# Sliding-window attention over bands of 192 keys per chunk, and the first output tile gated inside the stick-breaking stage

## The chip, the cores and the metric

The kernel runs on one core of a Trainium2 chip. The metric is the device time of one execution in microseconds (us), the median of several runs. A profile, taken by the hardware on one execution, gives for every instruction its engine, start and duration, and for every stretch the granted clock of TensorE. The engines are PE (TensorE matmul; its weight loads are shown apart as PEld), DVE (VectorE), ACT (ScalarE), POOL (GpSimd) and SP (SyncE, which here only issues DMAs).

## What is computed

One layer of a streaming encoder on 2048 prompt rows with 16 meta rows ahead of them, and 32 sample rows. The input projection gives the operands of three mixers (A, B, C) and a gate z; the mixers' outputs are joined, gated and projected back. The change touches mixer A (attention in which a chunk of 64 rows sees its own chunk and the two before it) and the joining at the end:

```
WIN_CHUNKS = WINDOW // CHUNK            # 128 // 64 = 2
def swa_prompt(q, k, v, sinks):
    ...
    band = lambda a: jnp.concatenate([a[:, j:j + n_c] for j in range(WIN_CHUNKS + 1)], axis=2)
    k_band = band(to_chunks(k))         # per chunk of 64 rows: 3 * 64 = 192 keys
    v_band = band(to_chunks(v))
    ...
    o = sink_attention(qc, k_band, v_band, sinks, ok)

def mixer_output(h, o_a, o_b, o_c, z, g_post, w_out):
    o = jnp.concatenate([o_a, o_b, o_c], axis=-1) * jax.nn.silu(z)
    return h + rmsnorm(jnp.einsum('btm,md->btd', o, w_out), g_post)
```

Mixer B is stick-breaking attention over all earlier rows, mixer C a gated delta rule.

## The kernel before, in words

The 2128 rows lie in 17 row tiles of 128 (TILES = 17, P = 128), so one tile holds two chunks of 64 (CH). The program is a row of stages, each with its own instruction streams per engine and a barrier between: the projection and convolution, the delta rule (both with side projections woven in), `window_attention`, `stick_breaking`, `output`. Within a stage the order of work on an engine is as written; engines meet by semaphores.

**`window_attention`** walks over `units` (m, s): row tile m (0 to 16, and 17 for the sample rows) and s, one of two sets of 4 heads, so 36 units. In step n, PE does `scores(n)`, `turn(n-3)` and `values(n-4)`. `scores` (L1474) first writes the mask of the window into PSUM `b_sc` by two matmuls of an identity with a mask table (L1486: 512 columns each, for two heads), then adds q times k for 4 heads (L1493: 64 contracted rows, 128 query rows, 256 keys, that is the row tile before and its own). DVE takes the row maximum (L1596) and forms the bias `nm` (L1600) and `se` (L1603); ACT does the exponentials with their sums, one per head (L1554), POOL multiplies by the reciprocal sum (L1580), PE turns the probabilities on their side (L1510, 128x128, 8 per unit) into `b_pt`, ACT (L1565) and DVE (L1626) copy one half each of that into `pt`, and `values` multiplies by v (L1524) into `b_o`, which DVE copies out per row tile (L1631). DVE's order in step n is maximum, `nm` and `se` of unit n, copy of unit n-3, then the sum and the reciprocal (L1610, L1614) of unit n-1, which release POOL. In fp32 each product is issued as two passes, a transpose as one.

**`stick_breaking`** runs 92 steps; in each, PE makes scores (L1816), transposes (L1839) and value products (L1854), ACT a sigmoid (L1907) and copies (L1921), DVE two scans (L1967). POOL only stores finished blocks of 4 row tiles into the scratch tensor `mix` (L1939). Towards its end SP loads `w_out` piece by piece into `w_raw` (L1788), a view of `base`.

**`output`** takes 17 row tiles through: SP loads the tile's `mix` and `sz` (gate) columns and the residual (L2047, L2048, L2056); ACT makes sigmoid(z) (L2089), POOL z times it (L2159), DVE gates `mixed` (L2128), ACT and DVE split the result into a high and a low part (`mhi` L2094, `mlo` L2132), and PE makes 48 passes of 512 columns (L2078). The weights are split likewise at the stage's start, k by k (`whi` L2115, `wlo` L2147), with the work on tile 0 written in between:

```
for k in range(KT):
    act.activation(whi[:, k, :], w_raw[:, k, :], ACT.Copy).then_inc(w_hi, 1)
    if k == SPLIT0 - 1:
        z_sigmoid(0, 0, 0)
    if k == SPLIT0:
        high(0, 0, 0)
z_sigmoid(1, 1, 0)
steps(act, step)
```

From then on ACT's `step` for tile n is z_sigmoid(n+2), a table load, high(n+1), and the normalisation of tile n.

Of the kernel before, what the change touches and what calls it, by code (L numbers as in the profile page):

```python
# [62 lines left out]
M_ID, M_DT, M_A0, M_A1, M_A, M_B = 0, 128, 192, 320, 576, 832  # L63
# [3 lines left out]
def shape_constants():  # L67
# [22 lines left out]
    cb[:, M_A:M_A + 2 * P] = np.where(win, 0, NEG)  # L90
# [6 lines left out]
def stream_layer(nc, io):  # L97
    top = ExitStack()
    with top:
# [24 lines left out]

        u_first = base_flat[:, 0:5 * P].rearrange("p (k t) -> p k t", k=5)
# [1273 lines left out]
        def window_attention():  # L1399
# [3 lines left out]
            with ExitStack() as st:  # L1403
# [5 lines left out]
                pr = sb("pr", [P, 4, AG, 2 * P], st=st)  # L1409
                pt = sb("pt", [P, 2, 2, AG, P], st=st)  # L1410
# [15 lines left out]
                slots = [(j, u) for u in range(2) for j in range(AKV)]  # L1426
                N = len(units)
# [17 lines left out]
                with nc.Block() as block:  # L1445
                    @block.sync
                    def _(sp):
# [4 lines left out]
                        load_piece(0)  # L1452
                        sp.dma_start(kc[:, :], io["cache_a_k"][0, 0].rearrange("t h d -> t (h d)")).then_inc(cache_in, 16)
# [19 lines left out]
                    def _(pe):  # L1473
                        def scores(n):  # L1474
# [7 lines left out]
                            q0 = SROW if m == TILES else m * P  # L1482
                            for a in range(0, AG, 2):
                                if m < TILES:
                                    at = M_A0 if m == 0 else (M_A1 if m == 1 else M_A)
                                    pe.matmul(b_sc[:, n % 2, a:a + 2, 0:K], identb, wide(cb[:, at:at + K], 2), start=True, stop=False,  # L1486
                                              skip_group_check=True)
# [12 lines left out]
                        def turn(n):  # L1500
# [3 lines left out]
                            if n:  # L1504
                                pe.wait_ge(pt_kept_act, n)
                                pe.wait_ge(pt_kept_dve, n)
                            for t, (_, part, k0) in enumerate(key_tiles(m, 0)):
# [5 lines left out]
                        def values(n):  # L1513
# [4 lines left out]
                            if n >= 4 and s == 0:  # L1518
                                pe.wait_ge(o_kept, n // 2 - 1)
                            heads = [key_tiles(m, j) for j in range(AKV)]  # L1520
# [128 lines left out]
        def stick_breaking():  # L1649
# [6 lines left out]
            TURN, VALUE = 3, 5  # L1656
            QS, KS = 0, 4
            with ExitStack() as st:
# [13 lines left out]
                krow = sb("krow", [P, 2, 2 * VBW], st=st)  # L1672
                spilled = [sem(f"spilled{b}", st) for b in range(NBLK)]
# [83 lines left out]
                with nc.Block() as block:  # L1757
                    @block.sync
                    def _(sp):
# [21 lines left out]
                        pieces += [(w_raw[:, k, :], wo[k * P:(k + 1) * P, :]) for k in range(AG, KT)]  # L1781
# [118 lines left out]
                    def _(act):  # L1900
# [15 lines left out]
                        for s in range(N + TURN):  # L1916
                            if s < N and s % 2 == 0:
# [330 lines left out]
```

## Time and profile before

| | us |
|---|---|
| runs | 1541.35, 1536.29, 1537.98 |
| median | 1537.98 |
| profiled execution, its own time | 1535.92 |
| its span, first to last instruction | 1534.2 |
| window_attention, about | 914.7 to 1047 |
| stick_breaking, about | 1051 to 1313 |
| output, about | 1317 to 1534 |

The page gives busy times per engine; the timeline gives start and duration of single instructions or of runs of like ones; the windows give the busy time of each engine in a stretch, with the granted clock (1.00 is 2.4 GHz, 0.50 is 1.2 GHz). A matmul's shown duration holds the pipeline's depth, so the rate of PE is read from start to start, not from durations.

### The profile page before, as it was taken

To read this page: it belongs to the slowest core of one execution; us is meant where nothing else is said; L and a number is where in the kernel's file an instruction comes from. 1 tells how busy PE (TensorE), PEld (TensorE's weight loads), DVE (VectorE), ACT (ScalarE), POOL (GpSimd) and SP (SyncE) were. 2 spreads that over 40 slices of the span, in tenths; PEclk is the share of its full clock that TensorE was granted. 3 is DMA by queue.
4 is the path that set the end of the run, shared out by engine and by line. 5 is a ranking of instruction groups with operands and counts; after the bars stand their busy time and mean duration, and the time that the engine had idled before them with its cause. 6 is when DMAs were issued, how large, how long until landed. Compare 5 with 4: busy or idle time off the path is not lost. (4 is left out here: it accounts for less than half of the span.)

```text
span 1534.2 us, 31162 instructions
## 1 busy us (share of the span) xinstructions
PE 1438.6 (94%) x12700; PEld 1196.5 (78%) x12700; DVE 792.2 (52%) x1507; ACT 640.9 (42%) x1440; POOL 383.8 (25%) x364
## 2 busy tenths in 40 slices
PE   6999998879999999999999979997999999599996
PEld 5999998868888888888888965554666666487785
DVE  5665566313334333335333327776788887444442
ACT  4455455411222112113111117674666676455551
POOL 0022223212212222223222114551000000255553
PEclk9999999899999999999999989998999999799998
DMA  8554446394243244433344423133000014656651
GB/s 249 169 149 130 142 124 160 106 224 135 83 132 97 68 117 125 127 94 96 110 126 126 121 73 120 64 102 94 15 15 2 15 33 122 189 158 170 201 177 62
DMA packets 202224, 177.36 MB, mean 116 GB/s; under 512 B 30114, under 2 KB 187879, under 8 KB 202087
## 3 DMA queue, kind: packets, MB, share of 16 engines
q1 hardware_dynamic: 153385, 117.86, 26.1%
q0 software_dynamic: 28256, 46.42, 10.9%
q10 hardware_dynamic: 20446, 11.14, 2.9%
q8 instruction: 99, 1.62, 0.4%
q14 instruction: 38, 0.31, 0.1%
HBM read 107.92 MB, written 65.59 MB: 113 GB/s over the span
## 5 line engine op out<-in xcount | busy, mean ns | idle before, releaser
L817 PE MATMUL acc<-side_rows,side_w 128*128 128x384 f32 (+2 forms) x2448 | 457.4, 335 | 15.9 <-ACT side_stage L836 7.7
L817 PEld LDWEIGHTS acc<-side_rows,side_w 128*128 128x128 f32 x2448 | 393.0, 191 | 33.3 <-ACT side_stage L836 7.8
L1967 DVE TENSOR_TENSOR_SCAN prod<-keepb,prod 128x512 f32<-128x512 f32 (+4 forms) x184 | 195.6, 1104 | 52.6 <-ACT keepb L1907 45.1
L709 PE MATMUL acc<-side_rows,side_w 128*128 128x384 f32 (+1 forms) x864 | 149.3, 330 | 0.0
L1276 DVE COPY base<-b_two 128x256 f32<-128x256 f32 x85 | 36.1, 424 | 212.9 <-PE b_two L1067 212.9
L709 PEld LDWEIGHTS acc<-side_rows,side_w 128*128 128x128 f32 x864 | 142.4, 188 | 1.9
L836 ACT ACTIVATE side_stage<-acc 128x384 f32<-128x384 f32 (+2 forms) x102 | 46.8, 461 | 211.4 <-PE acc L817 186.9
L2078 PE MATMUL b_y<-whi,mhi 128*128 128x512 f32 x272 | 107.4, 395 | 20.6 <-DVE mlo L2132 20.5
L1921 ACT ACTIVATE wt<-b_w 128x512 f32<-128x512 f32 (+5 forms) x188 | 88.0, 521 | 61.2 <-PE b_w L1839 61.1
L2078 PE MATMUL b_y<-whi,mlo 128*128 128x512 f32 x272 | 106.4, 391 | 0.0
L2078 PE MATMUL b_y<-wlo,mhi 128*128 128x512 f32 x272 | 106.4, 391 | 0.0
L1001 POOL TENSOR_TENSOR base<-base,ors 128x256 f32<-128x256 f32 x17 | 10.4, 611 | 334.9 <-ACT ors L1232 334.9
L1183 ACT ACTIVATE base<-b_dr 128x256 f32<-128x256 f32 x85 | 32.5, 383 | 144.5 <-PE b_dr L1059 144.5
L1907 ACT ACTIVATE keepb<-b_z 128x1024 f32<-128x1024 f32 (+4 forms) x92 | 79.7, 890 | 30.1 <-PE b_z L1816 18.9
L994 POOL TENSOR_TENSOR base<-base,cf 128x256 f32<-128x256 f32 x102 | 72.3, 743 | 79.2 <-DVE base L1257 79.2
L1839 PE MATMUL b_w<-cf,prod 128*128 128x128 f32 (+1 forms) x624 | 87.4, 280 | 3.1 <-ACT wt L1921 2.0
L1816 PE MATMUL b_z<-reg 64*128 64x512 f32 (+3 forms) x360 | 85.1, 575 | 4.4 <-PEq L2191 4.4
L1839 PEld LDWEIGHTS b_w<-cf,prod 128*128 128x128 f32 (+1 forms) x624 | 66.9, 142 | 27.2 <-issue 23.3
L1854 PE MATMUL b_o<-wt,vrow 128*64 128x128 f32 x1224 | 78.5, 278 | 6.5 <-DVE reg L1974 6.5
L1580 POOL TENSOR_TENSOR pr<-pr,rd 128x1024 f32<-128x1024 f32 (+2 forms) x36 | 65.1, 1809 | 68.5 <-ACT pr L1554 53.9
L2078 PEld LDWEIGHTS b_y<-whi,mhi 128*128 128x128 f32 x272 | 51.4, 189 | 34.6 <-DVE mlo L2132 19.5
L1854 PEld LDWEIGHTS b_o<-wt,vrow 128*64 128x64 f32 x1224 | 66.4, 137 | 15.0 <-issue 13.7
(230 smaller groups left out, 2345.9 us busy)
## 6 DMA issues: line engine op xcount, KB each, us to landing
side_rows<-hs_scratch POOLq DMA_DIRECT2D x16, 1536.0 KB, 10.3
hs_scratch<-side_rows SPq DMA_DIRECT2D x34, 512.0 KB, 4.7
mixed<-mix_scratch SPq DMA_DIRECT2D x17, 512.0 KB, 6.5
gates<-sz_scratch SPq DMA_DIRECT2D x17, 512.0 KB, 8.1
side_rows<-hs_scratch POOLq DMA_DIRECT2D x6, 1344.0 KB, 10.6
base<-in_x_prompt SPq DMA_DIRECT2D x15, 512.0 KB
xres<-in_x_prompt SPq DMA_DIRECT2D x15, 512.0 KB
out_y_prompt<-yy POOLq DMA_DIRECT2D x15, 512.0 KB, 6.5
```

The costliest lines, as they stand in the source:

```text
L709: last = pe.matmul(acc[:, u % 2, 0:w], side.w[:, c, w_, k, :], h_[:, b % 2, k, 0:w], start=(k == 0 and p == 0), stop=(k == KT - 1 and p == 2))
L817: last = pe.matmul(self.acc[:, n % 2, 0:width], w[:, w_part, k, :], rows[:, row_part, k, 0:width], start=(k == 0 and i == 0), stop=(k == K ...
L836: act.activation(self.stage[:, n % 2, 0:width], self.acc[:, n % 2, 0:width], ACT.Copy).then_inc(self.staged, 1)
L994: pool.tensor_tensor(atl[:, l], at[:, :, :], wide(lvl(l), 4), ALU.mult).then_inc(level, 1)
L1580: pool.tensor_tensor(x, x, rd[0:R, n % 4, :].unsqueeze(2).to_broadcast([R, AG, K]), ALU.mult).then_inc(normed, 1)
L1816: last = pe.matmul(b_z[0:R, s % 2, hh, 0:nk], reg[half, QS + a, q0:q0 + R], reg[half, KS + a, k0:k0 + nk], start=True, stop=not masks, ski ...
L1839: last = pe.transpose(b_w[0:kn, hh, t, 0:R], prod[0:R, hh, c0 + at:c0 + at + kn], ident[0:R, 0:R])
L1854: last = pe.matmul(b_o[hh * CH:hh * CH + CH, rowno[s] % 2, 0:R], v, wt[part, s % 4, hh, t, 0:R], start=(first and t == 0), stop=(last_ and ...
L1907: act.activation(keepb[0:R, s % 2, :, 0:nk], b_z[0:R, s % 2, :, 0:nk], ACT.Sigmoid, scale=-SCALE).then_inc(keep_ready, 1)
L1921: keep_weights(act, s - TURN, hh, lambda o, i: act.activation(o, i, ACT.Copy))
L1967: dve.tensor_tensor_scan(prod[0:R, hh, c0:c0 + nk][:, ::-1], kv, kv, prod[0:R, hh, c0 + nk:c0 + nk + 1], ALU.mult, ALU.bypass).then_inc(pr ...
L2078: last = pe.matmul(b_y[:, s, cols], m_[:, s, k, :], w_[:, k, cols], start=(k == 0 and p == 0), stop=(k == KT - 1 and p == 2))
```

## The change

Two things. For row tiles 2 to 16 ("banded", 30 of the 36 units) `window_attention` no longer computes 128 queries against 256 keys with a mask; each half tile (chunk c of 64 queries) is multiplied with its own band of 192 keys, which needs no mask. The scores become 8 products of 64 contracted rows, 64 query rows and 192 keys, one in each of the four quarters of the array for u and again; the transposes become 8 of 64 rows into 128x64 and 8 of 64 rows into 64x64; the values become, for each chunk, two products with 128 contracted rows and two with 64. Chunk 1's last 64 keys lie in partitions 64 to 127 of `vrow`, so a copy `v_low` in partitions 0 to 63 is made by one DMA at the stage's start. ACT's exponentials, DVE's maximum and POOL's product work on 192 instead of 256 columns per head. Tiles 0, 1 and the sample keep the old form.

Second, row tile 0 of the output is gated in `stick_breaking`: SP loads its `sz` and, once block 0 is stored, its `mix` columns into parts of `w_raw` not yet filled; ACT makes the sigmoid in step 41 (GATE), POOL two products of 128x1024. The last of the 8 pieces of `w_out` (k = 7) is loaded only in `output`, after tile 0 is split. `output` starts with high(0) and low(0), its first load is tile 1's, and PE does tile 0 k by k for both column halves.

```
 def window_attention():
+                v_low = sb("v_low", [CH, TILES, P], st=st)
...
+                b_band = b_pt[:, :, :, :].rearrange("p c g k -> p c (g k)").rearrange("p c (t g k) -> p c t g k", t=2, g=AG)
...
                 def keys(m):
-                    return P if m == 0 else (WIN + NSAMP if m == TILES else 2 * P)
+                    return P if m == 0 else (WIN + NSAMP if m == TILES else (2 * P if m == 1 else BAND))
...
                         load_piece(0)
+                        sp.dma_start(v_low[:, :, :], vA[CH:P, :, 0:P]).then_inc(low_in, 16)
...
+                            if banded(m):
+                                for u in range(2):
+                                    for c in range(2):
+                                        for j in range(AKV):
+                                            k0 = (m - 1) * P + c * CH
+                                            last = pe.matmul(b_sc[halves[c], n % 2, 2 * j + u, 0:BAND], reg[half[j], 2 * s + u, q0 + c * CH:q0 + (c + 1) * CH],
+                                                             reg[half[j], 4, k0:k0 + BAND], start=True, stop=True)
+                                last.then_inc(scores_ready, 1)
+                                return
...
+                            if banded(m):
+                                for g in range(AG):
+                                    for c in range(2):
+                                        pe.transpose(b_band[:, c, 0, g, :], pr[halves[c], n % 4, g, c * CH:c * CH + P], ident[halves[c], halves[c]])
+                                for g in range(AG):
+                                    for c in range(2):
+                                        k0 = 0 if c else P
+                                        last = pe.transpose(b_band[0:CH, c, 1, g, :], pr[halves[c], n % 4, g, k0:k0 + CH], ident[halves[c], halves[c]])
...
+                                for c in range(2):
+                                    for j in range(AKV):
+                                        pe.matmul(b_o[halves[j], m % 2, 2 * s:2 * s + 2, halves[c]], vA[:, m - 1 + c, halves[j]],
+                                                  p_band[:, n % 2, c, 0, 2 * j:2 * j + 2, :], start=True, stop=False)
+                                    for j in range(AKV):
+                                        rest = v_low[:, m - 1, halves[j]] if c else vA[0:CH, m, halves[j]]
+                                        last = pe.matmul(b_o[halves[j], m % 2, 2 * s:2 * s + 2, halves[c]], rest,
+                                                         p_band[0:CH, n % 2, c, 1, 2 * j:2 * j + 2, :], start=False, stop=True)
 def stick_breaking():
+            GATE = 41
...
+                        sp.dma_start(gate_raw, sz[:, :, 0:P].rearrange("k p t -> p k t")).then_inc(first_in, 16)
+                        sp.wait_ge(first_stored, 16)
+                        sp.dma_start(gated_first, mix[:, :, 0:P].rearrange("k p t -> p k t")).then_inc(first_in, 16)
+                        sp.wait_ge(first_gated, 1)
...
                         for s in range(N + TURN):
+                            if s == GATE:
+                                act.wait_ge(first_in, 32)
+                                act.activation(gate_sig, gate_raw, ACT.Sigmoid).then_inc(first_sig, 1)
...
                             store_outputs(b, 4 * (b + 1))
+                            if b == 1:
+                                pool.wait_ge(first_sig, 1)
+                                pool.tensor_tensor(gate_raw, gate_raw, gate_sig, ALU.mult).then_inc(first_silu, 1)
+                                pool.wait_ge(first_silu, 1)
+                                pool.tensor_tensor(gated_first, gated_first, gate_raw, ALU.mult).then_inc(first_gated, 1)
 def output():
...
+                            if exact(n) and n == 0:
+                                load(*ahead(1))
+                                sp.wait_ge(m_lo, 1)
+                                sp.dma_start(w_raw[:, KT - 1, :], io["w_out"][0][(KT - 1) * P:KT * P, :]).then_inc(w_last_in, 16)
+                                sp.dma_start(gpost[:, :], io["norm_post"].to_broadcast([P, D])).then_inc(gpost_in, 16)
+                            elif not exact(n) or n > 1:
+                                load(n, s, q)
+                            load_x(n, s, q)
...
+                        high(0, 0, 0)
                         for k in range(KT):
+                            if k == KT - 1:
+                                act.wait_ge(w_last_in, 16)
                             act.activation(whi[:, k, :], w_raw[:, k, :], ACT.Copy).then_inc(w_hi, 1)
-                            if k == SPLIT0 - 1:
-                                z_sigmoid(0, 0, 0)
-                            if k == SPLIT0:
-                                high(0, 0, 0)
-                        z_sigmoid(1, 1, 0)
+                            if k == SPLIT1:
+                                z_sigmoid(1, 1, 0)
```

How this stands on the engines: first PE in the middle of `window_attention`, one step of the loop before (scores, turn, values; a row is output, inputs and the product's shape):

```order
L1486 MATMUL b_sc<-cb 128x512 x2
L1493 MATMUL b_sc<-reg 128x256 x4
L1510 MATMUL b_pt<-cf,pr 128x128 x8
L1524 MATMUL b_o<-pt,vrow 64x256 x4
L1486 MATMUL b_sc<-cb 128x512 x2
```

and the same step now:

```order
L1499 MATMUL b_sc<-reg 64x192 x8
L1530 MATMUL b_pt<-cf,pr 128x64 x8
L1534 MATMUL b_pt<-cf,pr 64x64 x8
L1555 MATMUL b_o<-pt,vrow 64x2x64 x2
L1559 MATMUL b_o<-pt,vrow 64x2x64 x2
L1555 MATMUL b_o<-pt,vrow 64x2x64 x2
L1559 MATMUL b_o<-pt,v_low 64x2x64 x2
```

The 18 instructions of a step have become 32, the two of the mask are gone, and the values now go to and fro between 128 contracted rows (L1555) and 64 (L1559).

ACT at the start of `output`, before:

```order
L2115 ACTIVATE whi<-base 128x1024 x5
L2089 ACTIVATE zsig<-gates 128x1024
L2115 ACTIVATE whi<-base 128x1024
L2094 ACTIVATE mhi<-mixed 128x1024
L2115 ACTIVATE whi<-base 128x1024 x2
L2089 ACTIVATE zsig<-gates 128x1024 x2
L2109 ACT_TABLE_LOAD
L2094 ACTIVATE mhi<-mixed 128x1024
```

and now:

```order
L2172 ACTIVATE mhi<-base 128x1024
L2196 ACTIVATE whi<-base 128x1024 x6
L2166 ACTIVATE zsig<-gates 128x1024
L2196 ACTIVATE whi<-base 128x1024 x2
L2166 ACTIVATE zsig<-gates 128x1024
L2187 ACT_TABLE_LOAD
L2172 ACTIVATE mhi<-mixed 128x1024
```

Tile 0's sigmoid is gone and its high part stands first; the high part of tile 1 still stands behind the sigmoid of tile 2 and a table load.

SP at the start of `output`, before:

```order
L2047 DMA mixed<-mix_scratch 128x8x128
L2048 DMA gates<-sz_scratch 128x8x128
L2051 DMA xres<-in_x_prompt 64x1024
L2061 DMA gpost<-in_norm_post 128x1024
L2047 DMA mixed<-mix_scratch 128x8x128
L2048 DMA gates<-sz_scratch 128x8x128
L2056 DMA xres<-in_x_prompt 128x1024
L2047 DMA mixed<-mix_scratch 128x8x128
L2048 DMA gates<-sz_scratch 128x8x128
```

and now:

```order
L2108 DMA mixed<-mix_scratch 128x8x128
L2109 DMA gates<-sz_scratch 128x8x128
L2126 DMA base<-in_w_out 128x1024
L2127 DMA gpost<-in_norm_post 128x1024
L2114 DMA xres<-in_x_prompt 64x1024
L2119 DMA xres<-in_x_prompt 128x1024
L2108 DMA mixed<-mix_scratch 128x8x128
L2109 DMA gates<-sz_scratch 128x8x128
```

The first pair is tile 1's now, the second tile 2's; one pair less and the last piece of the weights more stand ahead of the gates of tile 2.

## Rows read from the trace of the kernel before

**Rows 1.** The page: busy us, share of the span and instructions of each engine.

```profile
PE 1438.6 (94%) x12700; PEld 1196.5 (78%) x12700; DVE 792.2 (52%) x1507; ACT 640.9 (42%) x1440; POOL 383.8 (25%) x364
```

**Rows 2.** Windows: stretch, its length, busy us of each engine, granted clock, DMA share, GB/s.

```profile
940.00:968.40 28.40, 28.40 (x206) 16.99 (x206) 20.80 (x52) 19.37 (x78) 15.14 (x8) 1.00 0.04 15
...
1160.00:1180.00 20.00, 20.00 (x188) 13.59 (x186) 17.16 (x18) 13.10 (x20) 0.00 (x0) 1.00 0.01 2
...
1313.50:1331.00 17.50, 0.00 (x0) 0.00 (x0) 9.37 (x9) 9.19 (x10) 3.03 (x2) 0.60 0.80 218
1331.00:1343.00 12.00, 11.97 (x47) 9.83 (x48) 5.51 (x4) 4.96 (x5) 6.14 (x2) 0.87 0.74 197
```

**Rows 3.** Timeline of PE in window_attention: start us, duration, engine, line, operation, count.

```profile
926.44 0.60 PE L1486 MATMUL b_sc<-cb 128*128 128x512 bf16 x2 [0.46 <-ACT pr L1554]
...
968.82 0.61 PE L1486 MATMUL b_sc<-cb 128*128 128x512 bf16 x2
...
969.36 1.13 PE L1493 MATMUL b_sc<-reg 64*128 64x256 f32 x8
...
970.42 1.09 PE L1510 MATMUL b_pt<-cf,pr 128*128 128x128 f32 x8
...
971.45 1.08 PE L1524 MATMUL b_o<-pt,vrow 128*64 128x256 f32 x8
...
972.46 0.61 PE L1486 MATMUL b_sc<-cb 128*128 128x512 bf16 x2
...
1034.34 0.41 PE L1496 MATMUL b_sc<-kcT,reg 64*32 64x128 f32 x4
```

**Rows 4.** Instructions on the tile pr: duration ns min/median/max, first and last start, forms.

```profile
L1580 POOL TENSOR_TENSOR pr<-pr,rd x36: 1035/1892/1894, 919.8 to 1043.3; 128x1024 f32<-128x1024 f32 x32, 128x512 f32<-128x512 f32 x2, 32x640 f32<-32x640 f32 x2
```

**Rows 5.** Timeline of DVE and POOL at the end of window_attention.

```profile
1033.68 0.16 DVE L1600 SCALAR_TENSOR_TENSOR nm<-mx,nsink 128x4 f32<-128x4 f32 x1
...
1036.00 0.97 DVE L1600 SCALAR_TENSOR_TENSOR nm<-mx,nsink 32x4 f32<-32x4 f32 x1
...
1038.20 1.89 POOL L1580 TENSOR_TENSOR pr<-pr,rd 128x1024 f32<-128x1024 f32 x1 [1.24 <-DVE rd L1614]
...
1039.39 0.72 DVE L1600 SCALAR_TENSOR_TENSOR nm<-mx,nsink 32x4 f32<-32x4 f32 x1
```

**Rows 6.** Timeline of PE: quarters in the delta rule, halves in the other stages.

```profile
703.86 0.46 PE L1067 MATMUL b_two<-base 64*64 64x64 f32 x16
704.16 0.51 PE L1094 MATMUL b_s<-cx_S,qk_ring 64*64 64x64 f32 x11
...
1045.04 0.34 PE L1524 MATMUL b_o<-pt,vc 128*64 128x64 f32 x4
...
1045.31 0.33 PE L1524 MATMUL b_o<-pt,vrow 32*64 32x64 f32 x4
...
1290.41 1.97 PE L1854 MATMUL b_o<-wt,vrow 128*64 128x128 f32 x32
```

**Rows 7.** Timeline at the start of output.

```profile
1317.21 4.84 ACT L2115 ACTIVATE whi<-base 128x1024 fp32r<-128x1024 f32 x5 [5.68 <-PEq L2191]
...
1318.30 5.77 DVE L2147 TENSOR_TENSOR wlo<-base,whi 128x1024 fp32r<-128x1024 f32 x5 [5.12 <-ACT whi L2115]
...
1323.81 1.06 ACT L2089 ACTIVATE zsig<-gates 128x1024 f32<-128x1024 f32 x1 [1.76 <-DMA gates<-sz_scratch]
...
1324.96 2.33 POOL L2159 TENSOR_TENSOR gates<-gates,zsig 128x1024 f32<-128x1024 f32 x1 [10.76 <-ACT zsig L2089]
...
1331.03 0.80 PE L2078 MATMUL b_y<-whi,mhi 128*128 128x512 f32 x1 [18.15 <-DVE mlo L2132]
...
1334.69 1.06 ACT L2089 ACTIVATE zsig<-gates 128x1024 f32<-128x1024 f32 x1 [2.13 <-DMA gates<-sz_scratch]
...
1338.15 2.04 DVE L2132 TENSOR_TENSOR mlo<-mixed,mhi 128x1024 fp32r<-128x1024 f32 x1 [1.30 <-ACT mhi L2094]
...
1343.42 0.39 PE L2078 MATMUL b_y<-whi,mhi 128*128 128x512 f32 x1
```

More of the change, by code:

```diff
@@ L2011, in output @@
                 LOOPS = (TILES - 8) // 3
-                SPLIT0 = 5
+                SPLIT1 = 5
+                w_last_in = sem("w_last_in", st)
                 mixed, gates = (sb(n, [P, 3, KT, P], st=st) for n in ("mixed", "gates"))
@@ L2016, in output @@
                 exact = lambda n: isinstance(n, int)
+                landed = lambda s, q: 32 * q + (32 if s else 0)
                 def rows(ap, n, base):
@@ L2071, in step, with products @@
                             reuse(pe, normed, n)
-                            for c in range(2):
+                            def products(k, c):
                                 cols = slice(c * 512, (c + 1) * 512)
-                                for k in range(KT):
-                                    if exact(n) and n == 0 and c == 0:
-                                        pe.wait_ge(w_lo, k + 1)
-                                    for p, (m_, w_) in enumerate(((mhi, whi), (mhi, wlo), (mlo, whi))):
-                                        last = pe.matmul(b_y[:, s, cols], m_[:, s, k, :], w_[:, k, cols],
-                                                         start=(k == 0 and p == 0), stop=(k == KT - 1 and p == 2))
+                                for p, (m_, w_) in enumerate(((mhi, whi), (mhi, wlo), (mlo, whi))):
+                                    last = pe.matmul(b_y[:, s, cols], m_[:, s, k, :], w_[:, k, cols],
+                                                     start=(k == 0 and p == 0), stop=(k == KT - 1 and p == 2))
+                                return last
+                            if exact(n) and n == 0:
+                                for k in range(KT):
+                                    pe.wait_ge(w_lo, k + 1)
+                                    for c in range(2):
+                                        last = products(k, c)
+                            else:
+                                for c in range(2):
+                                    for k in range(KT):
+                                        last = products(k, c)
                             last.then_inc(y_ready, 1)
@@ L2143, in step @@
                             norm(*ahead(0))
+                        low(0, 0, 0)
                         for k in range(KT):
```

57 lines of the change are left out of this document (35 added, 22 removed).

## The prediction

> **What bounds the kernel now.** I read the page first: PE is busy for 94% of the span [rows 1], so the end is set by PE's queue nearly everywhere, and a step is worth what it takes off PE, as long as no other engine is late next. Then the windows: in the middle of window attention PE is busy all 28.4 of 28.4 us at full clock, while DVE, the busiest beside it, has 20.8 [rows 2]. The other place is the head of the output stage: for 17.5 us PE does nothing [rows 2]; its first product starts at 1331.03, 13.8 us after ACT began on the weights [rows 7]. The change works on these two places, and borrows from a third, stick-breaking, where PE is busy 20.0 of 20.0 us and DVE 17.2 [rows 2].
>
> One step of window attention, from start to start on PE [rows 3]: masks 0.54 (968.82 to 969.36), scores 1.06, transposes 1.03, values 1.01; together 3.64. The 30 units that the change rewrites begin with the masks at 926.44 and end where the sample's scores begin, 1034.34: 107.9 us, 3.60 each (the first three are shorter).
>
> **The masks** go: minus 0.54 per unit, certain.
>
> **The scores** are now 16 passes of 192 columns in quarters of the array. Before, 8 passes of 256, two halves abreast, took 1.06 with everything around them, 0.52 ns per column. If four quarters run abreast, 3072 columns take 3072 x 0.26 = 0.80; if only two do, 1.59. The delta rule shows quarters: 16 passes of 64 columns (L1067) start at 703.86 and the next group starts 0.30 later [rows 6], 0.29 ns per column with short passes, which is close to 0.26. I take 0.80.
>
> **The transposes** keep their 1024 columns (16 of 64 for 8 of 128), now in two row halves that may run abreast: 0.51 if they do, 1.03 if not. No row shows fp32 transposes of two halves side by side, and there are twice as many weight loads, so I take 0.70.
>
> **The values** keep their columns too: 16 passes of 128. The nearest row is stick-breaking's, the same shape, 32 passes in 1.97 [rows 6], so 0.99. But a unit now goes three times between 128 and 64 contracted rows. The price of such a change: at the sample's units four passes of 64 columns with 128 rows start at 1045.04 and the four with 32 rows 0.27 later [rows 6]; by the rate above those passes need 4 x 31 ns = 0.12, so 0.15 is the change of form. Three of them are 0.45, and I take 0.36 of it, since some are covered by weight loads that run ahead: 1.35 (ends 0.99 and 1.44).
>
> The Trainium skill, "TensorEngine Tiling (Array Packing)", section "Key Properties", says that changing the tiling mode drains TensorE, and speaks against this change; the 0.15 above agrees with it. By that rule alone the sum would be 1.44 for the values and 0.15 more before the transposes.
>
> PE per unit: 0.80 + 0.70 + 1.35 = 2.85 (ends 0.80 + 0.51 + 0.99 = 2.30 and 1.59 + 1.03 + 1.44 = 4.06).
>
> **What is late next in window attention** is a loop of DVE and POOL. At the end of the stage, where no masks stand in PE's queue, DVE's small `nm` takes 0.97 and 0.72 instead of 0.16 [rows 5], and ends with POOL's product: POOL runs from 1038.20 to 1040.09, `nm` ends at 1040.11. `nm` waits for POOL, and POOL waits for what DVE does after `nm` (`se`, copy, sum, reciprocal): from 1036.97 to 1038.20, 1.23. So a step can't be shorter than 1.23 + POOL's 1.89 + 0.02 = 3.14 before. POOL takes 1.89 for 1024 columns and 1.03 for 512 [rows 4], so 1.46 for 768: 2.71 after. That lies just under PE's 2.85; ACT's and DVE's own work shrink as well. I take 2.85 for the step, which PE sets, with 2.71 as the floor: 30 x 2.85 = 85.5, **minus 22.4** (minus 26.6 at the floor).
>
> **`v_low`** is one DMA of 64 x 17 x 512 bytes, 0.56 MB, put ahead of the cache and the later pieces in SP's queue. It is first needed four steps after the first banded scores, and what is queued behind it is needed in steps 2 and 4. At the 218 GB/s of the output's head [rows 2] it is 2.6 us; mostly covered by units 0 to 2: plus 0.3 (0 to 2.6).
>
> **The output's head.** Tile 0 no longer waits for its loads, sigmoid and gate. High part from 1317.21, 1.06; low part 1.2; the first `wlo` 1.2 more (`whi` and `wlo` come at 4.84 / 5 = 0.97 and 5.77 / 5 = 1.15 each [rows 7]); so PE starts at about 1320.7 instead of 1331.03. Tile 0 takes 12.4 (1331.03 to 1343.42 [rows 7]), needs a new k only every 1.5 us, and would end at 1333.1. But tile 1 isn't ready then: its high part stands behind the sigmoid of tile 2 on ACT, and that waits for the gates, which landed at 1334.69, 17.5 us after the first load was issued [rows 7]. Ahead of them stand 3.75 MB now instead of 4.25 (one pair of 0.5 MB less, one piece of weights more), so 15.4 us: 1332.6. From there to the end of `mlo` it was 5.5 (1334.69 to 1340.19 [rows 7]): tile 1 starts at 1338.1 instead of 1343.42, 5.3 earlier, not 10.3. And PE has then stood still for 5.0 us. In the head before, the clock fell while PE stood still (mean 0.60 over 17.5 us, thus 3.5 us at 2.4 GHz and the rest at 1.2), and after PE's restart 3.1 of 12 us ran at 1.2 GHz (mean 0.87) [rows 2], which costs half of that. I count it a second time, at tile 1: 1.5. Gain 5.3 - 1.5 = 3.8 (ends: 1.7 if the gates land no earlier, 6 with no fall of the clock). The later tiles follow PE by a chain that starts from PE's own ends, so the gain stays to the end.
>
> **In stick-breaking** the gate adds 1.06 on ACT (as at 1323.81 [rows 7]) and two products of 2.33 on POOL [rows 7], idle until then. SP's wait for POOL delays only stores and weights that are due much later; POOL's next store, of block 2, has time. DVE is another matter, since its scans read SBUF while POOL does: in window attention `nm` stood still for POOL [rows 5], and at the output `mlo` took 2.04 where `wlo` of the same size takes 5.77 / 5 = 1.15 [rows 7]. If both products hold DVE up fully, that is 4.7 us in a stage where DVE is idle 14% of the time; with ACT's 1.06 the ends are 0 and 5.7. I take 1.5, since PE, two to three steps behind the scores, uses up DVE's lead and idle time first. **Gate in all: minus 2.3.**
>
> **Sum.** -22.4 + 0.3 - 2.3 = -24.4. The profiled execution's own time is 1535.92, so 1511.5; the median of the runs lies 2.06 above that execution: **1513.5**.
>
> **Rivals.**
> 1. *Slower: parts of the array do not run abreast.* If only two quarters do, and the transposes go one by one, PE needs 4.06 per unit: 30 x 4.06 = 121.8, plus 13.9, and with the gate 1549.6. It decides from a PE sum of 3.60 per unit. Against it: the quarters of the delta rule [rows 6]. Chance 0.06.
> 2. *Changes of form eat the gain.* Scores four abreast, transposes one by one (1.03), values 1.44: 3.27, and 0.15 more at one edge of the group: 3.4 per unit, minus 5.9; with the rest 1530. For it: 32 instructions for 18. Against: in two row halves the scores already ran abreast. Chance 0.14, of which a third within 0.3%.
> 3. *The gate costs more than it gives.* Both POOL products stop the scans, 5.7 lost in stick-breaking against 3.8: plus 1.9, 1517.7. Chance 0.15. The Trainium skill, "SBUF — State Buffer", section "SBUF: two separate sides", has such a rule: a GpSimd operation and a VectorE one with two SBUF inputs exclude each other for the whole instruction, and the scan has two such inputs; `nm` above agrees.
> 4. *The step doesn't shrink with its columns.* POOL's product over four strips of 192 costs what 1024 contiguous columns cost, and the loop stays at 3.14: 94.2, minus 13.7; 1522. For it: no row has a time for strips with gaps between. Against it: the two sizes in [rows 4] scale with their columns, and the gaps are in the free dimension alone. Chance 0.07.
>
> **How the numbers follow.** The forecast has 0.58. A measurement of this kernel can tell 0.3%, 4.6 us, from no change. Faster by more: 0.58 + 0.15 + 0.07 + two thirds of 0.14 = 0.89; within: 0.05; slower: 0.06. The range reaches down to 1503 (loop at its floor, minus 26.6, gate at its best, minus 6, and 2 us in the median) and up to 1527 (PE at 3.25 per unit, minus 10.4, and the gate without gain); rival 1 and most of rival 2 stay outside.
>
> **What would show it.** In the profile after: the step in the middle of window attention about 2.85 from start to start; 16 passes of scores in 0.8, transposes in 0.7, values in 1.35; `nm` often ending with POOL's product, which takes 1.46; PE's first product of the output some 3.5 us after ACT's first instruction there (13.8 before), then a gap of about 5 us ahead of tile 1, with the clock down; the scans next to POOL's two products stretched. A step over 3.3 or under 2.7, a tile 1 that starts without a gap, or a stick-breaking stage longer by more than 5 us would make steps of this wrong.

## The result, and the profile after

The changed kernel takes 1512.41 us (median of 4 runs, 1510.33 to 1515.72) where the kernel before takes 1537.13 beside it (4 runs, 1535.9 to 1541.35): a ratio of 0.984, 95% interval 0.9824 to 0.9857. That is faster by 24.7 us; 1513.5 had been forecast, in a range of 1503 to 1527. The profiled execution has a span of 1508.7 us against 1534.2. The page's line of the engines, to be read against [rows 1] (busy us, share of the span, instructions):

```profile
PE 1416.8 (94%) x13360; PEld 1190.4 (79%) x13360; DVE 771.9 (51%) x1506; ACT 636.3 (42%) x1440; POOL 377.4 (25%) x365
```

PE is busy 21.8 us less and still for 94% of the span. By stage, each measured between the same first instructions on PE and ACT in both traces:

| stretch | before | after | difference |
|---|---|---|---|
| up to window attention | 914.8 | 915.1 | +0.3 |
| window attention, up to the first banded scores | 11.7 | 12.4 | +0.7 |
| the 30 banded units | 107.9 | 83.7 | -24.2 |
| the sample's units and the change to the next stage | 16.6 | 16.1 | -0.6 |
| stick-breaking | 266.2 | 268.6 | +2.4 |
| output, from ACT's first piece of it | 217.0 | 212.9 | -4.2 |

Windows of after (stretch, length, busy us of each engine with its instructions, granted clock, DMA share, GB/s): the middle of window attention, the place of the gate in stick-breaking, and two stretches of the output's head. They answer to [rows 2].

```profile
940.00:967.20 27.20, 27.09 (x480) 18.00 (x474) 25.72 (x66) 23.40 (x102) 14.66 (x10) 1.00 0.21 63
1130.00:1150.00 20.00, 18.46 (x185) 12.76 (x182) 19.72 (x18) 13.58 (x21) 5.54 (x2) 1.00 0.00 1
1295.80:1313.00 17.20, 13.41 (x48) 10.57 (x48) 11.54 (x10) 10.82 (x12) 6.01 (x2) 0.75 1.00 290
1313.00:1326.00 13.00, 9.52 (x35) 7.66 (x36) 4.87 (x4) 8.34 (x10) 8.60 (x4) 0.87 0.43 111
```

The 27.20 us of the first row hold ten banded steps. PE is full, as before, but DVE now stands at 25.7 of 27.2, where it had 20.8 of 28.4: two limits have come to lie side by side. One step on PE, from transposes to transposes (start, duration, engine, line, operation, tile form, which is the rows*columns of the array in use, shape, count):

```profile
962.48 0.47 PE L1530 MATMUL b_pt<-cf,pr 64*128 64x64 f32 x8
962.78 0.39 PE L1534 MATMUL b_pt<-cf,pr 64*64 64x64 f32 x8
963.10 0.44 PE L1555 MATMUL b_o<-pt,vrow 128*64 128x128 f32 x4
963.47 0.44 PE L1559 MATMUL b_o<-pt,vrow 64*64 64x128 f32 x4
963.84 0.44 PE L1555 MATMUL b_o<-pt,vrow 128*64 128x128 f32 x4
964.21 0.33 PE L1559 MATMUL b_o<-pt,v_low 64*64 64x128 f32 x2
...
964.23 0.39 PE L1499 MATMUL b_sc<-reg 64*64 64x192 f32 x2
...
965.22 0.47 PE L1530 MATMUL b_pt<-cf,pr 64*128 64x64 f32 x8
```

From start to start it is 2.74 instead of the 3.64 of [rows 3]: transposes 0.62 (962.48 to 963.10), values 1.13 (to 964.23, where the next scores start while the last values still run), scores 0.99 (to 965.22; from 964.44 on, alone, 14 passes in 0.78). POOL's product, which answers to [rows 4] (min/median/max ns), is the other limit:

```profile
L1623 POOL TENSOR_TENSOR pr<-pr,rd x36: 1033/1467/1893, 920.1 to 1018.6; 128x768 f32<-128x768 f32 x30, 128x512 f32<-128x512 f32 x2, 128x1024 f32<-128x1024 f32 x2, 32x640 f32<-32x640 f32 x2
```

1.47 for 768 columns. Its starts in the banded steps lie 2.71 to 2.74 apart, 2.72 in the mean, 0.02 less than PE's. The timeline of after at the output's head: ACT, DVE, POOL, and PE's last product of tile 0 and first of tile 1 (compare [rows 7]):

```profile
1295.83 1.06 ACT L2172 ACTIVATE mhi<-base 128x1024 fp32r<-128x1024 f32 x1 [6.02 <-PEq L2266]
...
1298.06 9.17 DVE L2227 TENSOR_TENSOR wlo<-base,whi 128x1024 fp32r<-128x1024 f32 x8
...
1303.61 5.89 POOL L2235 TENSOR_TENSOR gates<-gates,zsig 128x1024 f32<-128x1024 f32 x1 [10.85 <-ACT zsig L2166]
...
1311.74 1.06 ACT L2166 ACTIVATE zsig<-gates 128x1024 f32<-128x1024 f32 x1 [6.33 <-DMA gates<-sz_scratch]
...
1312.45 0.39 PE L2143 MATMUL b_y<-whi,mlo 128*128 128x512 f32 x1
...
1312.82 1.28 ACT L2187 ACT_TABLE_LOAD   x1
1314.11 1.06 ACT L2172 ACTIVATE mhi<-mixed 128x1024 fp32r<-128x1024 f32 x1
...
1315.20 1.23 DVE L2210 TENSOR_TENSOR mlo<-mixed,mhi 128x1024 fp32r<-128x1024 f32 x1 [4.34 <-ACT mhi L2172]
...
1316.48 0.50 PE L2143 MATMUL b_y<-whi,mhi 128*128 128x512 f32 x1 [3.65 <-DVE mlo L2210]
...
1318.05 0.63 PE L2143 MATMUL b_y<-whi,mhi 128*128 128x512 f32 x1
```

PE's first product of the output is at 1299.43, 3.6 us after ACT's first piece (13.8 before). The gap of 3.65 ahead of tile 1 is the one foreseen: the high part of tile 1 stands on ACT behind the sigmoid of tile 2, which waits 6.33 for its gates. Some 1.5 us into tile 1 the products double in spacing, 0.43 instead of 0.23; the clock was 0.87 in this window, and tile 1 took 12.7 us where the next took 10.9.

### The profile page after: what moved, and what is told of

The parts are those of the page before. It is cut to its first block and busy times, and to the rows that moved or that the text cites. A ratio compares the mean times of both kernels' runs of the same rounds, so it can differ in the third digit from the quotient of the medians.

```text
span 1508.7 us, 32486 instructions
## 1 busy us (share of the span) xinstructions
PE 1416.8 (94%) x13360; PEld 1190.4 (79%) x13360; DVE 771.9 (51%) x1506; ACT 636.3 (42%) x1440; POOL 377.4 (25%) x365
## 5 line engine op out<-in xcount | busy, mean ns | idle before, releaser
L2026 DVE TENSOR_TENSOR_SCAN prod<-keepb,prod 128x512 f32<-128x512 f32 (+4 forms) x184 | 199.5, 1126 | 50.8 <-ACT keepb L1958 43.2
L695 PE MATMUL acc_v<-wv_hi,side_rows 128*128 128x392 f32 x272 | 74.9, 347 | 2.8 <-DVE side_rows L541 2.1
```

The costliest lines, as they stand in the source:

```text
L695: last = pe.matmul(acc_v[:, 0:RV], h_[:, s, k, part], w_[:, k, :], start=(k == 0 and p == 0), stop=(k == KT - 1 and p == 2))
L2026: dve.tensor_tensor_scan(prod[0:R, hh, c0:c0 + nk][:, ::-1], kv, kv, prod[0:R, hh, c0 + nk:c0 + nk + 1], ALU.mult, ALU.bypass).then_inc(pr ...
```

## The experiments

The theory was the prediction's: a banded step is limited by PE and, close beneath, by the loop of DVE and POOL; the gate gains at the output's head what a gap and a fall of the clock leave of it, and costs something beside the scans. The rivals were that the gate costs as much as it gives, and that one of the two limits alone sets the step.

**The two halves apart.** e1 has the new `window_attention` with `stick_breaking` and `output` as before; e2 the reverse.

```
e1:  stick_breaking, output: the functions of the kernel before
+    gated_first = w_raw[:, KT - 1, :].rearrange("p (k t) -> p k t", k=KT)     (left in e1, not used there)
e2:  window_attention: the function of the kernel before
```

> Bands of 192 keys alone; stick-breaking and output as before. Theory A (the two parts are independent and the trace's split is right: window attention 24.0 us shorter, the gate worth 4.1 - 2.4 = 1.7 net): 24 us under the kernel before, a ratio near 0.984, with window attention about 112 us from its first product to stick-breaking's (136 before) and the other stages within 0.5 us of before. Rival B (part of the output's gain comes from the earlier stage, or the bands disturb what follows): a total that differs from 24 by more than 2 us.

> The gate of tile 0 in stick-breaking alone; window attention as before. Theory A: 1.7 us under the kernel before (2.4 lost in stick-breaking, 4.1 won in output), a ratio near 0.999, hardly told from 1. Rival B (the loss in stick-breaking belongs to the other part): 4 us under. Rival C (the gain at the output's head is given back later): no change or slower.

e1 took 1513.81 us, ratio 0.9859 (0.9841 to 0.9877), e2 1531.56, ratio 0.9972 (0.996 to 0.9984), against 1536.64 beside them. The bands give 22.8 us, as theory A had them (within 2 of 24). The gate alone gives 5.1, more than A's 1.7 and B's 4; together they'd be 27.9, but the changed kernel has 24.7. The stages say where the rest is: stick-breaking loses 1.9 in e2 (268.1) and nothing in e1 (266.4), so the gate costs there what after shows. The output shrinks by 6.6 in e2 (210.4) and by 4.2 in after. In e2 tile 1 starts 19.91 us after ACT's first piece, after a wait of 2.93, and takes 11.0: the granted clock stayed at 1.00. In after it starts at 20.65, after a wait of 3.65, and takes 12.7. So most of the difference of 2.4 between the two outputs, 1.7, is the clock in tile 1.

**POOL's share of the step.** e5 lets POOL multiply only 64 of the 192 columns, so the other probabilities stay unnormalised.

```
-    x = pr[0:R, n % 4, :, 0:K]
+    W = CH if 2 <= m < TILES else K
+    x = pr[0:R, n % 4, :, 0:W]
```

> The changed kernel in which POOL multiplies 64 of the 192 columns per head in the banded units (the other probabilities stay without the division by the sum: part of the computation is left out). POOL's product falls from 1.47 to about 0.65. If PE sets the step: it stays at 2.74, window attention at 112. If the loop of DVE and POOL sets it: nm is no longer held up and the step falls to what DVE needs itself, 2.5 to 2.6, window attention to 105 to 108.

The step stayed at 2.74. What changed is `nm`, the small instruction that follows DVE's maximum. The row of the instructions on `nm` in the middle of window attention in after (count, then min/median/max ns):

```profile
L1643 DVE SCALAR_TENSOR_TENSOR nm<-mx,nsink x25: 161/166/750, 941.6 to 1007.5; 128x4 f32<-128x4 f32 x25
```
and the same row in e5:

```profile
L1644 DVE SCALAR_TENSOR_TENSOR nm<-mx,nsink x26: 161/163/165, 940.9 to 1009.3; 128x4 f32<-128x4 f32 x26
```

With POOL's product at 0.61 us, `nm` is never held (165 ns at most), and the step is no shorter: PE's 2.74 holds it.

**PE's share of the step.** e4 groups the value products by form: all with 128 contracted rows, then all with 64. In this order the sums over the keys of a half are not kept whole, so part of the values is left out; it is read for its time.

```
     for c in range(2):
         for j in range(AKV): ... vA[:, m - 1 + c, halves[j]] ... start=True
+    for c in range(2):
         for j in range(AKV): ... rest ... stop=True
```

> The changed kernel with the values of a unit in another order: the four products with 128 contracted rows first, then the four with 64, so one change of form inside the values where there were three. Against the changed kernel's step of 2.74. If the loop of DVE and POOL is the floor (POOL's 1.47 and 1.25 between its product and the next nm): PE gains 2 x 0.16 but the step stays at 2.71 to 2.74, window attention at about 112. If PE alone sets the step: 2.42, window attention about 102 to 103. If the change of form costs nothing: 2.74 and the values take as long as now, 1.13 up to the next scores.

Here, too, the step hardly moved: 2.72. PE now waits 0.21 us at the transposes for DVE's copy of the step before, and `nm` is held in every second step, up to the end of POOL's product (the same row in e4):

```profile
L1644 DVE SCALAR_TENSOR_TENSOR nm<-mx,nsink x26: 161/457/754, 940.5 to 1009.1; 128x4 f32<-128x4 f32 x26
```

In after, too, `nm` is held in every second step, but for less and less: from 750 ns down to 166, as it must be where the loop needs 0.02 less than PE's step. In e4 it is held for 750 to 754 to the end. So each limit alone holds the step where it is: PE at 2.74, the loop at 2.72.

e4 and e5 ran once each, in 1516.48 and 1516.54 us, and the whole of window attention took 116.4 and 116.9 where about 112 had been expected. That isn't the banded units (83.0 and 83.3 us; 83.0 in e1, 83.7 in after) but what stands around them: the start took 15.2 and 16.6, which comes up again below, and the sample's units with the change of stage 18.2 and 17.0 instead of 16.1, which was not pursued.

**Both limits lifted.** e7 puts the value products in the order 64, 128, 128, 64 rows, which has two changes of form instead of four and adds up each half before the next begins, and lets DVE make the reciprocal ahead of its copy, so that POOL's product runs beside copy and maximum.

```
-    for c in range(2):                    # 128 rows, then 64, for each half
+    for c, wide_step in ((0, False), (0, True), (1, True), (1, False)):
+        opens = (c == 1) == wide_step
...
-    if 3 <= n < N + 3: keep(n - 3)
     if 1 <= n <= N: norm(n - 1)
+    if 3 <= n < N + 3: keep(n - 3)
```

> The changed kernel with both limits of the banded step lifted at once: TensorE's value products in the order 64, 128, 128, 64 rows (two changes of tile form instead of four, sums as before), and VectorE makes the reciprocal ahead of its copy of the transposed probabilities, so that GpSimd's product runs beside copy and maximum. Theory (a step is the larger of TensorE's 2.74 and the VectorE-GpSimd loop's 2.72, and nothing else is near): the step falls to 2.55 to 2.65 us and the stretch of window attention by 2 to 5 us against a run with the same start. Rival (a third limit, ScalarE with 2.30 busy and its wait of 0.42 for the bias): the step stays at 2.70 or more.

POOL's starts now lie 2.74 and 2.38 to 2.59 apart in turn (once 3.11), 2.62 in the mean, inside the 2.55 to 2.65 expected; the 30 units took 80.2 us instead of 83.7, and the one run 1505.64. One step on PE in e7, from its timeline:

```profile
961.17 0.46 PE L1530 MATMUL b_pt<-cf,pr 64*128 64x64 f32 x8
961.44 0.42 PE L1534 MATMUL b_pt<-cf,pr 64*64 64x64 f32 x8
961.79 0.44 PE L1562 MATMUL b_o<-pt,vrow 64*64 64x128 f32 x4
962.15 0.66 PE L1558 MATMUL b_o<-pt,vrow 128*64 128x128 f32 x8
962.74 0.33 PE L1562 MATMUL b_o<-pt,v_low 64*64 64x128 f32 x2
...
963.76 0.46 PE L1530 MATMUL b_pt<-cf,pr 64*128 64x64 f32 x8
```
and the row of `nm` in e7:

```profile
L1645 DVE SCALAR_TENSOR_TENSOR nm<-mx,nsink x27: 149/162/165, 941.3 to 1009.5; 128x4 f32<-128x4 f32 x26, 32x4 f32<-32x4 f32 x1
```

Eight passes of 128 rows in one group take 0.59 (962.15 to 962.74); in after the same eight took 0.37 twice. That prices a change of form at 0.15, as the prediction had it from the sample's units. The step shown fell by one such price, from 2.74 to 2.59, though two changes are gone: the one behind the transposes had cost nothing that could be seen (the sixteen transposes take 0.62 ahead of it in after, and 0.62 in e7 without it). `nm` is no longer held at all.

Stick-breaking was 2.8 us shorter in this run, though nothing in it was changed. 1.0 of it lies in its first 9 us, where the clock came back sooner (1.00 instead of 0.74 in the 5 us that begin some 5 us after the first product). Another 1.6 lie behind a wait of 2.12 for DVE's `reg`, which both kernels have; in after

```profile
1047.68 1.03 PE L1905 MATMUL b_o<-wt,vrow 128*64 128x128 f32 x12 [2.12 <-DVE reg L2033]
1048.64 1.97 PE L1890 MATMUL b_w<-cf,prod 128*128 128x128 f32 x8
1050.54 1.90 PE L1867 MATMUL b_z<-reg 64*128 64x512 f32 x8
```
and in e7:

```profile
1043.43 0.88 PE L1907 MATMUL b_o<-wt,vrow 128*64 128x128 f32 x12 [2.12 <-DVE reg L2035]
1044.24 1.09 PE L1892 MATMUL b_w<-cf,prod 128*128 128x128 f32 x8
1045.26 1.35 PE L1869 MATMUL b_z<-reg 64*128 64x512 f32 x8
```

The granted clock of this piece was 0.64 in after (1047.68 to 1052.37) and 1.00 in e7 (1043.43 to 1046.55). e10 below, with the same edit, shows the same; the other profiles all have the clock down here. What of the edit keeps it up is not shown.

**What the gate costs in stick-breaking.** e3 cuts POOL's two products of the gate to 8 columns; sigmoid and DMA stay.

```
-    pool.tensor_tensor(gate_raw, gate_raw, gate_sig, ALU.mult)
+    pool.tensor_tensor(gate_raw[:, 0, 0:8], gate_raw[:, 0, 0:8], gate_sig[:, 0, 0:8], ALU.mult)
...                                                    (and the second product likewise)
```

> The changed kernel with the two gate products that GpSimd makes during stick-breaking (2.38 and 3.16 us in the trace of after) cut to 8 columns; so the gate of output tile 0 is left out and tile 0 of the output is not the reference's. The sigmoid on ScalarE and the DMA stay. Theory (GpSimd's products hold VectorE's scans beside them, which took 6.53 us for four and 4.26 for two, and this makes the 2.4 us that stick-breaking lost): stick-breaking 268.6 -> 266.2 to 266.8 us. Rival (the sigmoid's 1.07 us on ScalarE, with what waits behind it there, makes the loss): stick-breaking stays at 268.2 to 268.8.

Stick-breaking fell from 268.6 to 266.9, in one run, slightly over the 266.2 to 266.8 of the theory and far from the rival's 268.2. The timeline of DVE and POOL around the gate in after:

```profile
1134.31 6.53 DVE L2026 TENSOR_TENSOR_SCAN prod<-keepb,prod 128x384 f32<-128x384 f32 x4
...
1137.38 2.38 POOL L2002 TENSOR_TENSOR base<-base 128x1024 f32<-128x1024 f32 x1 [29.42 <-ACT base L1970]
1139.84 3.16 POOL L2004 TENSOR_TENSOR base<-base 128x1024 f32<-128x1024 f32 x1
...
1141.01 4.26 DVE L2026 TENSOR_TENSOR_SCAN prod<-keepb,prod 128x512 f32<-128x512 f32 x2
```

and DVE's at the same place in e3:

```profile
1135.72 4.48 DVE L2026 TENSOR_TENSOR_SCAN prod<-keepb,prod 128x384 f32<-128x384 f32 x4
...
1141.66 2.46 DVE L2026 TENSOR_TENSOR_SCAN prod<-keepb,prod 128x512 f32<-128x512 f32 x2 [1.21 <-ACT keepb L1958]
```

Four scans of 384 columns take 6.53 beside POOL and 4.48 without it, two of 512 take 4.26 and 2.46. All scans of the stage, as the view that groups instructions by line has them in after (busy us, mean ns | idle us before):

```profile
L2026 DVE TENSOR_TENSOR_SCAN prod<-keepb,prod 128x512 f32<-128x512 f32 (+4 forms) x184 | 199.5, 1126 | 50.8 <-ACT keepb L1958 43.2 <-PE b_w L1890 4.6
```
and in e3:

```profile
L2026 DVE TENSOR_TENSOR_SCAN prod<-keepb,prod 128x512 f32<-128x512 f32 (+4 forms) x184 | 195.6, 1105 | 53.0 <-ACT keepb L1958 48.1 <-PE b_w L1890 1.9
```

DVE stood 3.9 us longer in its scans, and POOL's products took 5.54 instead of 4.66 (2.33 each, [rows 7]), 0.9 more: together 4.8, about what the products take alone, so the two engines hardly ran at the same time. The stage paid 1.7 of the 3.9, since DVE had idle time.

That 1.7 can be read without the rest of the stage. Between two fixed passes of its scores that enclose the gate (the 141st and the 181st of `b_z<-reg`) PE took 27.7 us in before, e1 and e3, and 29.4 in after, e2 and every other kernel with the whole gate. So POOL's products are all of the cost there, and the sigmoid and the DMAs, which e3 keeps, cost nothing that can be seen. The other 0.7 of after's 2.4 are not at the gate: 0.35 lie in the stage's first 10 us, where the clock came back later than in before (mean 0.76 instead of 0.84 in the second 5 us), and 0.3 behind the last scores.

**The order at the output's head.** e8 lets ACT make the high part of tile 1 ahead of the sigmoid of tile 2, in the first step only.

```
+    first = exact(ahead(0)[0]) and ahead(0)[0] == 0
+    if first: high(*ahead(1))
     if has(2): z_sigmoid(*ahead(2)); act.preload_act_table_set(LN_EXP)
-    if has(1):
+    if has(1) and not first:
         high(*ahead(1))
```

> The changed kernel, and in the first step of the output's loop ScalarE makes the high half of tile 1 before the sigmoid of tile 2, which waits 6.3 us for a DMA. Theory (the gap of 4.0 us ahead of tile 1, and the low granted clock that follows it, are made by that order alone): tile 1 starts 15.5 to 17.5 us after ScalarE's first piece of the output instead of 20.65, the clock stays high in it, and the output shrinks from 212.85 to 207 to 210 us. Rival (tile 1 is late for another reason, the gate of tile 1 on GpSimd beside VectorE): tile 1 starts at 19.5 or later and the output stays above 211.

1504.81 us in one run, and the output 207.5 instead of 212.9. The timeline of ACT and PE at the head of e8:

```profile
1310.44 1.06 ACT L2172 ACTIVATE mhi<-mixed 128x1024 fp32r<-128x1024 f32 x1 [5.19 <-DVE mixed L2209]
1311.85 1.06 ACT L2166 ACTIVATE zsig<-gates 128x1024 f32<-128x1024 f32 x1 [0.35 <-DMA gates<-sz_scratch]
...
1312.26 0.39 PE L2143 MATMUL b_y<-whi,mlo 128*128 128x512 f32 x1
1312.82 0.50 PE L2143 MATMUL b_y<-whi,mhi 128*128 128x512 f32 x1 [0.17 <-DVE mlo L2213]
```

and the window of e8 that answers to the last one of after (columns as there):

```profile
1313.00:1326.00 13.00, 13.00 (x58) 10.75 (x59) 3.90 (x4) 9.41 (x14) 8.78 (x4) 1.00 0.46 124
```

The wait ahead of tile 1 falls from 3.65 to 0.17, the clock stays at 1.00, and tile 1 starts at 17.15 and takes 11.0. The order alone made the gap, and with the gap went the fall of the clock.

**The copy `v_low`.** The start of window attention differed more than anything else from run to run: up to the first banded scores it took 12.4 us in after, 13.5 in e1, 14.1 in e7, 15.2 in e4 and 16.6 in e5, and 11.7 before. PE waits there for the second piece, which stands behind `v_low` in SP's queue. e9 moves the copy: its first four tiles behind the second piece, the rest behind the third.

```
-    sp.dma_start(v_low[:, :, :], vA[CH:P, :, 0:P])
...
     load_piece(i)
+    if i == 1: sp.dma_start(v_low[:, 0:4, :], vA[CH:P, 0:4, 0:P])
+    if i == 2: sp.dma_start(v_low[:, 4:TILES, :], vA[CH:P, 4:TILES, 0:P])
...                                                    (PE waits for the second part at row tile 5)
```

> The changed kernel with the copy of the values' lower rows (544 KB, 8.3 to 11.3 us on its queue) moved behind the pieces that the first steps wait for: a first part behind the second piece, the rest behind the third. Theory (that copy delays the second piece, so that TensorE waits for it 2.5 us in after and 3.6 to 5.5 in the other kernels with bands, against 1.7 before): that wait falls to 2 us or less, and the stretch of window attention from 112.2 (116.9 at most) to 109.5 to 111.5 us. Rival (the start is long for another reason, such as the clock): the stretch stays at 112 or more, or the wait passes on to the copy itself at the first banded values.

The waits of before and of after name PE's for that piece (us in total, times, longest):

```profile
PE b_sc L1486 <- DMA reg<-uT_scratch: 1.7, 1, 1.7
PE b_sc L1506 <- DMA reg<-uT_scratch: 2.5, 1, 2.5
```
the DMA issues of after have the copy (KB, us from issue to landing):

```profile
v_low<-vrow SPq DMA_DIRECT2D x1, 544.0 KB, 8.3
```
and the waits of e9 the same wait:

```profile
PE b_sc L1509 <- DMA reg<-uT_scratch: 1.4, 1, 1.4
```

The wait falls below the 1.7 of the kernel before, and the stretch up to the first banded scores to 11.4; PE doesn't wait for the copy itself. The whole of window attention fell by 0.2 only, to 112.0 (one run, 1511.23 us): the theory's 109.5 to 111.5 was missed, and the 112 of the rival reached. Of the 1.0 won at the start, 0.3 is lost in the 30 units and 0.5 behind them, and the profiled execution of after has one of the shortest starts of all kernels with the copy at the old place, which left e9 little to gain. What e9 is worth shows in the next two.

**All three together.** e10 has the edits of e7, e8 and e9; e11 is the changed kernel again, beside it.

```
     after + value order and reciprocal of e7 + high part first of e8 + v_low of e9
```

> The changed kernel with the three edits of the earlier runs together: value products in the order 64, 128, 128, 64 rows with VectorE's reciprocal ahead of its copy; ScalarE's high half of tile 1 ahead of the sigmoid of tile 2; the copy of the lower value rows behind the pieces that the first steps need. Theory (they stand in three different stretches and add up): 2.5 to 4 us from the banded steps and the start together, 5 us from the output, so 1503 to 1506 us, ratio to the kernel before 0.978 to 0.980. Rival (a gain in one stretch moves the granted clock in the next and is given back): above 1507 us, no better than the output edit alone, which was 7 us under the changed kernel in one look.

> The changed kernel as it is, beside the combined one on the same chip. Theory: 1510 to 1515 us as before. A time of 1508 or less would mean that the one looks at the other kernels were taken on a faster chip, and that their gains over the changed kernel are smaller than they seemed.

e10 took 1499.66 us (5 runs, 1497.12 to 1500.65), ratio 0.9754 (0.9739 to 0.9769) against 1537.0 before; e11 took 1512.14, ratio 0.9834 (0.9818 to 0.9851). So e10 lies 12.5 us under the changed kernel, more than the theory's 1503 to 1506, and the rival's giving back did not come. e11 lies in the 1510 to 1515 expected, so the gains of the single runs stand. By stages of e10 and of e11: start of window attention 11.1 and 15.1, the 30 units 79.9 and 84.0, stick-breaking 265.8 and 268.4, output 208.1 and 214.8. (The profiled execution of e11 took 1515.86, 3.7 over its median, so these differences add up to more than 12.5.) The 2.6 of stick-breaking stood in no theory; it is the clock, as in e7. In e11's profile the copy had again pushed the second piece back:

```profile
PE b_sc L1506 <- DMA reg<-uT_scratch: 4.8, 1, 4.8
```

With the copy at SP's head this stretch took 12.1 to 16.6 us in eight profiles, with it moved 11.1 and 11.4. PE's wait for the second piece goes with the copy's own time to landing: 2.5 at 8.3 (after), 3.6 at 9.2 (e1), 4.1 at 10.2 (e4), 4.8 at 10.6 (e11), 5.5 at 11.3 (e5). That the move removes the spread is likely from these rows; why the copy takes 7.7 us in one run (e8) and 11.3 in another isn't shown.

## Why the prediction was right, step by step

The time was met (1512.4 for 1513.5), by a sum whose terms were each a little off, in both directions. The mechanisms held; that the total is so near is partly luck, since the units gave more than forecast, and the copy and stick-breaking cost more.

- **The step.** 2.85 had been forecast, with a floor at 2.71; it came to 2.74. Scores 0.99 instead of 0.80, but with 0.2 of that beside the last values; transposes 0.62 for 0.70; values 1.13 for 1.35, since the last group runs under the next scores. The quarters do run abreast: 14 passes of 192 columns in 0.78 is 0.29 ns per column, as in the delta rule [rows 6], a little more than half of the 0.52 before. (The prediction's 0.99 for the values took the shown 1.97 of stick-breaking's row, which holds the pipeline's depth; from start to start those 32 passes take 1.90.) The 30 units gave 24.2 for the 22.4 forecast. Rivals 1 and 2 fell with this.
- **The loop.** 2.71 had been worked out from POOL's two sizes and DVE's 1.23; e4 shows 2.72, with POOL at 1.47 for the 1.46. Rival 4 fell. That both limits would lie within 0.02 of each other was not foreseen, and it is the reason why e4 and e5 gained nothing and e7 did. `nm` ended with POOL's product, as forecast.
- **The change of form.** 0.15 was right between the groups of the values (e7); the change behind the transposes, which the prediction did not count, showed no cost. The Trainium skill, "TensorEngine Tiling (Array Packing)", section "Key Properties", says that TensorE drains at a change of mode. The trace agrees between the groups of the values, where such a change costs 0.15.
- **`v_low`: the term that was mis-sized.** +0.3 had been taken, from its bytes at 218 GB/s, 2.6 us. The row says 8.3 from issue to landing (10.6 in e11), for 1088 packets of 512 bytes that moved beside other transfers. The stretch up to the first banded scores became 0.7 longer in the profiled execution, within the range of 0 to 2.6, but 3.5 longer in e11, outside it. What failed is the 2.6 for the copy, and with it "mostly covered by units 0 to 2": the second piece stands behind the copy and is needed in step 2, and PE waited 2.5 for it in after and 4.8 in e11, against 1.7 before. The total hid this: the units gave 1.8 more than forecast.
- **The output's head.** PE's start at 3.5, found 3.6; gates of tile 2 at 15.4, found 15.9; tile 0's end at 15.9, found 17.0, so that PE stood still for 3.65 instead of 5.0; tile 1 at 20.9, found 20.65; gain 5.3, found 5.56; minus 1.5 for the clock, found 1.8; in all 3.8, found 4.2. e8 shows that the gap comes from ACT's order alone and that the clock's part goes with it.
- **Stick-breaking.** 1.5 forecast, 2.4 found, within 0 to 5.7; 1.7 of it is POOL's products, the rest is not the gate. The Trainium skill, "SBUF — State Buffer", section "SBUF: two separate sides", has a GpSimd operation that reads SBUF and a VectorE one with two SBUF inputs exclude each other. The 4.8 us above agree with it. Rival 3 was right in its mechanism and wrong in what it takes from it: 3.9 us are lost on DVE, and the stage gives back over half of them.
- **The gate in all** was to give 2.3. It gave 1.8 by stages in the profiled execution, and 5.1 alone. In e11's profile it gave nothing: stick-breaking 2.2 longer than before, the output 2.2 shorter. Beside the bands its worth is thus 0 to 1.8 in these two profiles, and the bands make nearly all of the gain.

## What to carry to other kernels

When a change takes work off the engine that bounds a loop, work out the next limit from the same rows: here it lay 0.02 us below, and every further edit to one side alone was worth nothing that could be told. A small DMA that a change adds is priced by what stands behind it in its queue, and by how soon that is needed, not by its bytes alone. And an engine's queue at a stage's head deserves the same look as the loop: moving one instruction of ACT ahead of a wait gave 5 us, as much as the gate itself.

## What the runs showed of the hardware that was not expected

- The exclusion of DVE and POOL works both ways. At the output's head POOL's gate product took 5.89 us beside DVE's `wlo`, which ran on at 1.15 each, and ended 2.27 after the last of them; the same product takes 2.34 a little later, alone.
- A wait of 3.65 us between two tiles was followed by a clock at half level some 1.5 us after the restart; waits of 2.93 (e2) and 0.17 (e8) were not. The six other profiles with bands and gate, and ACT's order as in after, had waits of 3.5 to 4.1, and tile 1 took 12.6 to 13.5 there. What else differs between after and e2 here was not separated.
- 32 fp32 instructions in three tile forms in a step of 2.74 us leave PE busy 27.09 of 27.20 us: no idle time came with the 32 instructions in place of 18. That need not be PE's full rate: the columns of the scores took 0.29 ns, where half of the 0.52 before would be 0.26.
